# Interleaving the high and low parts of the stationary activations in an encoder layer on one Trainium2 core

## The reference, cut to what matters

```python
D_MODEL, SEQ, D_FF, N_HEADS = 2048, 256, 5632, 16
x = x + 0.5 * swiglu_ffn(rms_norm(x, ffn1_norm_g), ffn1_w_gate, ffn1_w_up, ffn1_w_down)
h = rms_norm(x, mix_norm_g)
u = h @ w_in                      # conv (4096), q (768), kv (512), k_rope (64), two gates (2048 each)
y_conv = conformer_conv_branch(u_conv, ...)      # 31 taps per channel, layer norm, then @ conv_w_pw_out
y_mla = mla_branch(c_q_raw, c_kv_raw, ...)       # 16 heads over latents of 768 and 512, then @ mla_w_o
merged = sigmoid(gl_conv) * y_conv + sigmoid(gl_mla) * y_mla
x = x + merged @ w_out
x = x + 0.5 * swiglu_ffn(rms_norm(x, ffn2_norm_g), ffn2_w_gate, ffn2_w_up, ffn2_w_down)
return rms_norm(x, final_norm_g)
```

## Time and profile before

| what | value |
|---|---|
| median of 3 runs | 2327.15 us (2326.44 to 2562.85) |
| profiled execution, its time | 2326.71 us |
| profiled execution, its span | 2324.8 us |
| PE busy | 2299.0 us, 99% |
| PEld busy | 1924.4 us, 83% |
| DVE busy | 1322.2 us, 57% |
| ACT busy | 1188.3 us, 51% |
| DMA | 432.65 MB, mean 186 GB/s |

### The profile page before, as it was taken

The page is one execution under the profiler, slowest core; times in us unless marked ns, Lnnn a source line. Parts: engine busy times, 40 slices in busy tenths (PEclk is TensorE's granted clock), DMA queues, the critical chain, the costliest instruction groups (busy, mean ns, idle before and its releaser), DMA issues.

```text
span 2324.8 us, 26788 instructions
## 1 busy us (share of the span) xinstructions
PE 2299.0 (99%) x10718; PEld 1924.4 (83%) x10718; DVE 1322.2 (57%) x1470; ACT 1188.3 (51%) x1620; POOL 0.2 (0%) x4
## 2 busy tenths in 40 slices
PE   8999999999999999999999999999999999999997
PEld 7888888888888888878889888888888888888886
DVE  5544544544545488997875465555544544544443
ACT  6444444444444577787776564444444444444443
POOL 0000000000000000000000000000000000000000
PEclk9999999999999999999999999999999999999999
DMA  8666666666665665566643455656666666666664
GB/s 289 189 190 190 190 185 196 190 187 192 190 191 187 186 199 183 171 198 182 199 136 119 138 174 185 189 184 208 188 186 196 191 186 189 191 188 193 195 191 135
DMA packets 121532, 432.65 MB, mean 186 GB/s; under 512 B 13632, under 2 KB 13888, under 8 KB 121280
## 3 DMA queue, kind: packets, MB, share of 16 engines
q1 hardware_dynamic: 121408, 430.93, 60.0%
HBM read 428.78 MB, written 2.10 MB: 185 GB/s over the span
## 4 chain that ended last, share of the span: by engine, by line
PE 97%; DVE 1%; ACT 1%; issue 1%; DMA 0%; SPq 0%; ACTq 0%; DVEq 0%
PE bank L682 31%; PE bank L684 31%; PE bank L683 31%; PE turned L693 2%; PE bank L825 1%; PE bank L799 1%; PE bank L800 1%; DVE q_rope L1117 0%; PE turned L810 0%; ACT w_hi L432 0%; DVE w_lo L927 0%; DVE q_rope L1123 0%; DMA raw<-in_ffn_up 0%; PE turned L879 0%; ACT q_rope L540 0%
## 5 line engine op out<-in xcount | busy, mean ns | idle before, releaser
L927 DVE TENSOR_TENSOR w_lo<-raw,w_hi 128x1024 fp32r<-128x1024 f32 (+2 forms) x814 | 986.9, 1215 | 954.8 <-ACT w_hi L432 954.5
L432 ACT ACTIVATE w_hi<-raw 128x1024 fp32r<-128x1024 f32 (+2 forms) x814 | 853.0, 1051 | 998.4 <-PE bank L684 987.9
L682 PE MATMUL bank<-w_hi,h 128*128 128x512 f32 (+1 forms) x2144 | 835.9, 390 | 10.1 <-DVE w_lo L927 10.1
L684 PE MATMUL bank<-w_hi,h 128*128 128x512 f32 (+1 forms) x2144 | 832.7, 388 | 0.0
L683 PE MATMUL bank<-w_lo,h 128*128 128x512 f32 (+1 forms) x2144 | 832.6, 388 | 0.0
L682 PEld LDWEIGHTS bank<-w_hi,h 128*128 128x128 f32 x2144 | 403.0, 188 | 92.7 <-DVE w_lo L927 11.4
L684 PEld LDWEIGHTS bank<-w_hi,h 128*128 128x128 f32 x2144 | 402.9, 188 | 83.1
L683 PEld LDWEIGHTS bank<-w_lo,h 128*128 128x128 f32 x2144 | 403.1, 188 | 81.6
L682 PE MATMUL bank<-w_hi,hidden 128*128 128x512 f32 x704 | 274.3, 390 | 0.0
L684 PE MATMUL bank<-w_hi,hidden 128*128 128x512 f32 x704 | 273.9, 389 | 0.0
L683 PE MATMUL bank<-w_lo,hidden 128*128 128x512 f32 x704 | 273.9, 389 | 0.0
(11 more groups left out here) (171 smaller groups left out, 1223.4 us busy)
## 6 DMA issues: line engine op xcount, KB each, us to landing
raw<-in_ffn_up SPq DMA_DIRECT2D x352, 512.0 KB, 4.1
raw<-in_ffn_down SPq DMA_DIRECT2D x176, 512.0 KB, 3.6
raw<-in_conv_in SPq DMA_DIRECT2D x64, 512.0 KB, 3.8
raw<-in_conv_gate SPq DMA_DIRECT2D x32, 512.0 KB, 4.2
raw<-in_mla_gate SPq DMA_DIRECT2D x32, 512.0 KB, 4.2
raw<-in_mla_out SPq DMA_DIRECT2D x32, 512.0 KB, 3.6
raw<-in_conv_out SPq DMA_DIRECT2D x32, 512.0 KB, 3.7
raw<-in_w_out SPq DMA_DIRECT2D x32, 512.0 KB, 3.6
```

The source lines that it names most:

```text
L432: act.activation(w_hi[:, j, 0:n], raw[:, j, 0:n], ACT.Copy).then_inc(hi_ready, 1)
L682: pe.matmul(dst, fixed_hi, moving_hi, start=first, stop=False)
L684: return pe.matmul(dst, fixed_lo, moving_hi, start=False, stop=last)
L927: dve.tensor_tensor(w_lo[:, j, 0:n], raw[:, j, 0:n], w_hi[:, j, 0:n], ALU.subtract).then_inc(lo_ready, 1)
```

## The change

For `h`, `hidden`, `attn` and `merged` the last two dimensions change places: a high word and its low word now lie side by side, and the 256 tokens of one part have a step of two words. Every write of a part and every weight load from these four goes through `one_part` or `part_of_tile`, with the new step. A load's 128 columns are spread over 1024 bytes in place of 512. `c_kv` and `c_q` keep their layout. `before_hidden` grows from 248 to 264 words, so that everything behind it (`hidden`, `attn`, `merged`, `c_kv`, `c_q` and others) lies 64 bytes further; `h`, `w_hi`, `w_lo` and `raw` stay. No instruction is added, removed or moved on any engine, no wait changes, and sizes, counts and streamed operands of all wide matmuls are the same.

```diff
-        h = sb("h", [P, KT, 2, T], F32R)
+        h = sb("h", [P, KT, T, 2], F32R)
...
-        sb("before_hidden", [P, 248])
+        sb("before_hidden", [P, 264])
...
-        hidden = sb("hidden", [P, FT, 2, T], F32R, outs)
+        hidden = sb("hidden", [P, FT, T, 2], F32R, outs)
...
-        attn = sb("attn", [P, KT, 2, T], F32R, outs)
+        attn = sb("attn", [P, KT, T, 2], F32R, outs)
...
-        merged = sb("merged", [P, KT, 2, T], F32R)
+        merged = sb("merged", [P, KT, T, 2], F32R)
...
+        latents = (c_kv, c_q)
+
+        def one_part(buffer, k, n):
...
+            return buffer[:, k, n, :] if buffer in latents else buffer[:, k, :, n]
+
+        def part_of_tile(buffer, k, n, tt):
...
+            tokens = slice(tt * P, (tt + 1) * P)
+            return buffer[:, k, n, tokens] if buffer in latents else buffer[:, k, tokens, n]
...
-                        act.activation(dst[:, k:k + 2, 0, :], pair, ACT.Copy).then_inc(turn_hi, 1)
+                        act.activation(one_part(dst, slice(k, k + 2), 0), pair, ACT.Copy).then_inc(turn_hi, 1)
...
-                        tokens = slice(tt * P, (tt + 1) * P)
-                        last = multiply(banks(g)[tt][:, 0:w], (fixed[:, k, 0, tokens], fixed[:, k, 1, tokens]), moving,
-                                        k == 0, k == g.deep - 1)
+                        last = multiply(banks(g)[tt][:, 0:w], (part_of_tile(fixed, k, 0, tt), part_of_tile(fixed, k, 1, tt)),
+                                        moving, k == 0, k == g.deep - 1)
...
-                        dve.tensor_tensor(dst[:, k:k + 2, 1, :], pair, dst[:, k:k + 2, 0, :],
+                        dve.tensor_tensor(one_part(dst, slice(k, k + 2), 1), pair, one_part(dst, slice(k, k + 2), 0),
                                           ALU.subtract).then_inc(turn_lo, 1)
```

More of the change, by code:

```diff
@@ L497, in take_turns @@
                         for r in range(2):
-                            act.activation(dst[:, k + r, 0, :], pair[:, r, :], ACT.Copy,
+                            act.activation(one_part(dst, k + r, 0), pair[:, r, :], ACT.Copy,
                                            scale=gain[col][:, k + r, :]).then_inc(turn_hi, 1)
@@ L569, in attend_out @@
                 for j in range(2):
-                    act.activation(attn[:, 2 * p + j, 0, :], out_bank[:, j * T:(j + 1) * T], ACT.Copy).then_inc(head_hi, 1)
+                    act.activation(one_part(attn, 2 * p + j, 0), out_bank[:, j * T:(j + 1) * T], ACT.Copy).then_inc(head_hi, 1)
             def keep_keys(s):
@@ L620, in _ @@
                     for k in range(DEEP * u, DEEP * (u + 1)):
-                        act.activation(h[:, k, 0, :], xt[:, k, :], ACT.Copy, scale=gain["ffn1"][:, k, :]).then_inc(xt_hi, 1)
+                        act.activation(one_part(h, k, 0), xt[:, k, :], ACT.Copy, scale=gain["ffn1"][:, k, :]).then_inc(xt_hi, 1)
                 round_unit(u)
@@ L1064, in take_turns @@
                         for r in range(2):
-                            dve.scalar_tensor_tensor(out=dst[:, k + r, 1, :], in0=pair[:, r, :], scalar=gain[col][:, k + r, :],
-                                                     in1=dst[:, k + r, 0, :], op0=ALU.mult,
+                            dve.scalar_tensor_tensor(out=one_part(dst, k + r, 1), in0=pair[:, r, :], scalar=gain[col][:, k + r, :],
+                                                     in1=one_part(dst, k + r, 0), op0=ALU.mult,
                                                      op1=ALU.subtract).then_inc(turn_lo, 1)
@@ L1170, in split_channels @@
                 two = active[:, 2 * (n % 2):2 * (n % 2) + 2, :]
-                dve.tensor_scalar(h[:, 2 * n:2 * n + 2, 0, :], two, 1.0, None, ALU.mult).then_inc(ln_hi, 1)
+                k = slice(2 * n, 2 * n + 2)
+                dve.tensor_scalar(one_part(h, k, 0), two, 1.0, None, ALU.mult).then_inc(ln_hi, 1)
                 dve.wait_ge(ln_hi, n + 1)
-                dve.tensor_tensor(h[:, 2 * n:2 * n + 2, 1, :], two, h[:, 2 * n:2 * n + 2, 0, :],
+                dve.tensor_tensor(one_part(h, k, 1), two, one_part(h, k, 0),
                                   ALU.subtract).then_inc(ln_lo, 1)
@@ L1182, in _ @@
                         dve.wait_ge(xt_hi, k + 1)
-                        dve.scalar_tensor_tensor(out=h[:, k, 1, :], in0=xt[:, k, :], scalar=gain["ffn1"][:, k, :],
-                                                 in1=h[:, k, 0, :], op0=ALU.mult, op1=ALU.subtract).then_inc(xt_lo, 1)
+                        dve.scalar_tensor_tensor(out=one_part(h, k, 1), in0=xt[:, k, :], scalar=gain["ffn1"][:, k, :],
+                                                 in1=one_part(h, k, 0), op0=ALU.mult, op1=ALU.subtract).then_inc(xt_lo, 1)
                 if part == 0 and 1 <= s <= PAIRS:
```

2 lines of the change are left out of this document (1 added, 1 removed).

## The result

| | before | changed kernel |
|---|---|---|
| median | 2326.8 us | 2381.57 us (2381.12 to 2382.53) |
| ratio, 95% interval | | 1.0236 (1.0224 to 1.0249) |
| span of the profiled execution | 2324.8 us | 2379.3 us |
| step of an `h` product, 512 columns | 226.7 ns | 233.3 ns |

The change makes the kernel 2.4% slower. The forecast was 2235 us, 92 us faster; the measured time lies outside the range, 46.6 us above its upper end of 2335, and nearest to the rival "slower", at less than half of its price of 124 us.

A forecast was written before the change was run, and what follows sets the result against it. TensorE's pace, 226.7 ns per wide matmul, was taken as the bound. Cheaper loads would save 97 us and the taps' stretches give back 5, so 92 us off 2326.7, stated as 2235 us; range 2213 to 2335.

The forecast's parts named there:

- slower: Rival for loads with two words' step: more hold-ups or half read rate, step about 240 ns, 2451 us; chance 0.18.
- What bounds the kernel: Whole kernel: TensorE's pace, 226.7 ns per 512-column matmul, sets the time, except in the convolution taps' stretch.
- The 13.3 ns: Wide matmuls: excess over 213.3 ns of columns, put down to weight load and full-rate stream disturbing each other in memory.
- The price of a load with a step of two words: Loads from h, hidden, attn, merged: 10.4 ns less each, step 216.3 ns, times 9312 is 97 us less.
- The bounds: Loads with two words' step: between all 13.3 ns gone, 124 us less, and cost doubled to 26.7 ns, 124 us more.
- nearest to: Plain float32 products, 216.3 ns a pass, taken as the nearest row where a load disturbs nobody.
- The 64 bytes: Shift of hidden, attn and merged against the streamed words: taken for nothing, kept as a rival.
- only `h` gains: Rival: the shifted buffers' position is the bad one, so h's products alone gain, 67 us less 5, 2265 us; chance 0.08.
- the forecast's own range: Whole kernel: steps from 214.5 to 219.5 ns with 3 to 8 us given back, stated as 2213 to 2262 us.
- No change: Rival for wide products: 13.3 ns belong to any 128-word load wherever it lies, 2327 us; 0.20 together with a milder form.
- The rule against it: Skill's statement on TensorE's two independent read ports: a load's step could not matter, time would stay 2327 us.
- Writes, cold start, transfers: Writes with two words' step: no change, some microseconds at worst at the start; lower-clock loads cost nothing; transfers need 198 GB/s.

The follow-up runs named there:

- step alone: The changed kernel with the gap before hidden put back to 248 words, so only the loads' step of two words remains: 2386.46 us, ratio 1.0257.
- the stream in turns: Kernel before, with the wide products' streamed operand read one word from either half alternately, weights laid out for it: 2228.35 us, ratio 0.9576; changed kernel likewise: 2227.96 us.
- the last small kernel: No layer computation, only streams of 100 matmuls with loads, some of just 128 or 64 columns; 128 columns with step-one loads took 111 ns a step.

## Why the prediction was wrong

**What bounds the kernel: right.** TensorE's step set the time in all seven versions of the layer's kernel, and nothing else did but for some microseconds in the taps.

**The 13.3 ns arise between load and stream: right in the main, in part shown.** The cost changes with the load's place, step and form, and it was seen only while the stream takes words at 2.4 per ns; that all of it comes from the load stays unshown, as said above. Changing how the stream is read, with loads and words untouched, takes 10.9 of the 13.3 ns away and leaves 2.5, near the 2.9 of the earlier trace rows. The estimate of what the disturbance costs in all, 10.4 ns x 9312 = 97 us, came out at 98.7 us (2327.01 less 2228.35, with 9384 products), only not by this change.

**The price of a load with a step of two words: the step that failed.** The term was -10.4 ns, a step of 216.3; measured +6.7 ns, 233.3. Over 9312 loads that is -97 us forecast against +59.8 us (step alone). Its premise held: the last paragraph of the prediction said it would be wrong if the load's real pace were far above 4.3 bytes per ns, and the pace is 4.6, with a step of two 8.6 against the stream's 9.6. The inference fell: "two readers at one pace that have got out of each other's way stay so". A load that stands still on one word (231.7) disturbs about as much as one that keeps up with the stream (233.3), and one with a step of three, which in turns fits into 215.8, somewhat more (235.6). (The 246.7 of a step of eight say little on this: 240 of them are the load's own length.) Difference of pace is not what makes them meet. The bounds were sound, 213.3 to 240, and the value was taken at the wrong end: the row it was "nearest to", has a stream at half the words per ns, which is another case, not a nearer one. The two rows with a stream at full rate, 226.7 and 232 behind a break, said that undisturbed pairs don't occur there, and the second of them, taken for support, showed that the step could well become 232.

**The 64 bytes: wrong.** Taken for nothing, since loads 512 bytes apart have one step. They cost 17.7 us alone, and give some 5 us back beside a step of two. A place that doesn't matter between 0 and 512 is one sample of a pattern that repeats every 256 bytes; the kernel before had all its buffers at the best place that was tried for 512 columns. The rival "only `h` gains, because the other position is the bad one" had its premise right for a step of one, and no gain to apply it to.

**The sums.** One slip is in the forecast's own range: steps of 214.5 and 219.5 ns with 3 to 8 us given back are 2216 and 2268 us, not 2213 and 2262. And the pair of writes for `hidden` stands beside 96 matmuls, not 48. Neither bears on the outcome.

**The rivals.** "No change" fell with its reason: the 13.3 ns are no fixed hold-up for so many words. "Slower" was the right side with a wrong mechanism: neither doubled meetings (+6.7, not +13.3 ns) nor a load at half rate (118 to 120 ns, not 240). The threshold that it named, 5 ns more per load for a time 2% slower, is what decided. It should have had more than 0.18: since the price of a new pattern could lie on either side of 226.7, and the only row for it was one from another rate, there was nothing to give the lower side three times the chance of the upper.

**The rule against it.** That TensorE's two read ports keep a load from taking bandwidth from the running matmul, as the Trainium skill has it (TensorE: Matmul & The Clock Gate, Step-by-step: what each phase is for), is contradicted by these runs: 226.7, 230.0 or 233.3 ns by where the load's words lie. The N / 2.4 + 2.5 of the same page of the Trainium skill (Back-to-back issue gap), given there for a matmul by itself, is what the stream in turns reaches, 215.8, 135.8 and, with a load as the bound as well, 111.7 ns at 256 columns where the formula has 109.2. The Trainium skill's rule of two hits per 16-byte line (SBUF — State Buffer, Door 1: The DMA port swizzle) fails on both sides for TensorE's stream: one with exactly two hits per line takes 451 ns, and one that changes the line with every word 215.8.

**Writes, cold start, transfers: right.** Writes of two k-tiles of `hidden` went from 584 to 619 ns on ScalarE and 682 to 684 ns on VectorE, all hidden; the first microseconds have the same step.

## What to carry to other kernels

A price for an access pattern that the trace does not show is unknown in sign, whatever model of the contention makes it plausible; a hundred matmuls with constant addresses measure it in 25 us. In float32r products that load 128 columns for each matmul, look at the step between starts: 226.7 ns at 512 columns is not the floor, and reading the streamed operand in turns of one word between its two halves, with the weights laid out for it, gave 4.2% of the whole kernel. When one step is the kernel, the distance of every stationary buffer from the streamed one modulo 256 bytes is part of the tuning, and a buffer grown ahead of it can cost as much as the 0.75% here.

## What the runs showed of the hardware

- The step of a float32r matmul with one load depends on the distance of its two operands in memory modulo 256 bytes: 226.7 to 234.3 ns at 512 columns with a load of step one, 230.0 to 235.6 with a step of two, 117.3 to 120.0 at 256 columns, and in opposite sense (place 0, best for 512 columns, is the worst of the five tried for 256). In the layer's kernel one place and step can have two steps, 230.0 and 233.3, before and behind a break.
- A load of 128 words takes 112 ns, with a step of two 118 to 120 ns, of four 233, of eight 240; with three it fits into 215.8 ns and with six into 225.0.
- A stream with a step of two words runs at half pace (451 ns), one in turns between two places at full pace and freed of the load (215.8), one in turns among four places at 283, among sixteen at 435.
- In the last small kernel the granted clock fell from 1.00 to 0.50, the lower of its two levels, during streams of 128 columns, though TensorE and its loads were busy all the time. Windows of that kernel (us, busy PE, PEld, DVE, POOL, clock, DMA share, GB/s):

```profile
40.00:60.00 20.00, 20.00 (x176) 19.92 (x175) 0.00 (x0) 0.00 (x0) 1.00 0.00 1
60.00:66.00 6.00, 6.00 (x41) 6.00 (x41) 0.00 (x0) 0.00 (x0) 1.00 0.00 0
68.00:80.00 12.00, 12.00 (x53) 12.00 (x53) 0.00 (x0) 0.00 (x0) 0.50 0.01 1
80.00:100.00 20.00, 20.00 (x85) 20.00 (x86) 0.00 (x0) 0.00 (x0) 0.50 0.00 0
...
240.00:260.00 20.00, 20.00 (x144) 20.00 (x144) 0.00 (x0) 0.00 (x0) 0.80 0.00 1
```

  Before it fell the engine ran 128 columns every 112 to 118 ns, still at 1.00, and from 63.2 us on 128 columns every 233 ns (loads with a step of four); the clock fell in that stream. It rose at 248 us, in the first stream of 256 columns, which until then had one every 213 ns and from then on one every 112. A PE that is 100% busy in the profile is thus no sign that the clock will stay.

Open is why the map of places and steps looks as it does, why one place and step has now 230.0 and now 233.3, why a load that stands still disturbs as much as a moving one, and why turns between two places free the stream while turns among four don't. These were measured, and no model here explains them.
